# Two-layer decoder trunk on one core: scale row applied in the normalization, evictions rounded straight from the bank, loop-end products by column halves

## What is computed

```python
mod = silu(c) @ ada_w[i] + ada_b[i]
sh_a, sc_a, g_a, sh_f, sc_f, g_f = split(mod, 6)
h = rmsnorm(x, norm_mix[i]) * (1.0 + sc_a) + sh_a
x = x + g_a * mixer(h)
h = rmsnorm(x, norm_ffn[i]) * (1.0 + sc_f) + sh_f
x = x + g_f * moe(h)
```

## Time and profile before

| | |
|---|---|
| median of 3 runs | 1396.59 us (1392.68 to 1397.88) |
| profiled execution | 1399.82 us |
| its span | 1398.1 us |
| PE busy | 1323.5 us, 95% |
| DVE busy | 548.5 us, 39% |
| ACT busy | 454.5 us, 33% |
| POOL busy | 226.3 us, 16% |
| HBM read | 514.11 MB, 369 GB/s over the span |
| granted PE clock, mean | 0.983 |

### The profile page before, as it was taken

How to read it: one execution, slowest core, us unless ns; L and a number is a source line. 1 busy time by engine, 2 the same in 40 slices (tenths; PEclk the granted TensorE clock), 3 DMA queues, 4 the chain that set the end, 5 groups by cost and what they waited for, 6 DMA issues and landing times.

```text
span 1398.1 us, 33554 instructions
## 1 busy us (share of the span) xinstructions
PE 1323.5 (95%) x12029; PEld 877.8 (63%) x12030; DVE 548.5 (39%) x1263; ACT 454.5 (33%) x926; POOL 226.3 (16%) x684
## 2 busy tenths in 40 slices
PE   5899989999999999899899999999999999999986
PEld 2788675556565555445699898765555565555653
DVE  1665684323332322222644365753323233233324
ACT  3444552222222222112544554622222222222222
POOL 8200102111111211111200000021111111112110
PEclk9899999999999999999999999999999999999998
DMA  9998989999999999999996344599999999999994
GB/s 352 338 338 319 404 358 400 420 421 422 422 422 422 422 422 422 422 422 422 376 351 216 126 151 151 203 402 383 422 423 421 422 422 422 422 422 421 422 421 199
DMA packets 113979, 516.09 MB, mean 369 GB/s; under 512 B 10280, under 2 KB 47264, under 8 KB 64000
## 3 DMA queue, kind: packets, MB, share of 16 engines
q1 hardware_dynamic: 109920, 509.64, 91.0%
q0 software_dynamic: 3296, 3.50, 0.9%
q10 hardware_dynamic: 704, 2.10, 0.4%
HBM read 514.11 MB, written 1.09 MB: 369 GB/s over the span
## 4 chain that ended last, share of the span: by engine, by line
PE 65%; SPq 17%; DMA 9%; DVE 4%; ACT 2%; issue 2%; ACTq 0%; DVEq 0%
PE bank L980 17%; PE bank L1169 13%; SPq L352 8%; PE bank L1136 7%; PE bank L1095 6%; PE bank L1172 6%; PE bank L1197 6%; DMA ring<-in_exp_w_dram 6%; SPq L355 4%; PE bank L1203 3%; SPq L346 3%; DMA mods<-in_exp_w_dram 2%; PE bank L954 2%; DMA ring<-in_da_w_in_dram 2%; DVE ring_r L1472 1%
## 5 line engine op out<-in xcount | busy, mean ns | idle before, releaser
L1169 PE MATMUL bank<-ring,arena 128*64 128x512 f32 x768 | 183.9, 614 | 13.1 <-DMA ring<-in_exp_w_dram 13.1
L1136 PEld LDWEIGHTS bank<-arena 128*128 128x128 bf16 x3264 | 142.1, 98 | 55.5 <-issue 55.5
L1095 PE MATMUL bank<-arena_r 128*128 128x512 f32 x560 | 159.9, 422 | 3.0 <-DVE arena_r L1648 3.0
L1641 DVE SCALAR_TENSOR_TENSOR arena<-bank,arena 128x128 f32<-128x128 f32 x103 | 32.9, 348 | 327.5 <-ACT arena L749 327.5
L1648 DVE TENSOR_TENSOR arena_r<-bank,arena_r 128x512 fp32r<-128x512 f32 x136 | 94.1, 692 | 154.1 <-ACT arena_r L756 154.1
L1136 PE MATMUL bank<-arena 128*128 128x64 bf16 (+1 forms) x3264 | 151.8, 207 | 0.0
L749 ACT ACTIVATE arena<-bank 128x256 f32<-128x256 f32 (+1 forms) x68 | 22.6, 332 | 387.8 <-PE bank L1169 280.2
L566 POOL TENSOR_TENSOR arena<-arena,pass_base 128x2 f32 x136 | 26.2, 216 | 736.9 <-PE bank L1144 569.8
L756 ACT CAST arena_r<-bank 128x512 fp32r<-128x512 f32 x136 | 79.6, 586 | 175.3 <-PE bank L1197 112.4
L1169 PEld LDWEIGHTS bank<-ring,arena 128*64 128x64 f32 x768 | 69.0, 141 | 107.5 <-issue 101.6
L980 PE MATMUL bank<-HH_r,ring_r 128*128 128x256 f32 x448 | 127.2, 284 | 0.0
(11 more groups left out here) (277 smaller groups left out, 2168.6 us busy)
## 6 DMA issues: line engine op xcount, KB each, us to landing
ring<-in_exp_w_dram SPq DMA_DIRECT2D x264, 1024.0 KB, 24.6
ring<-in_ada_w_dram SPq DMA_DIRECT2D x48, 1024.0 KB, 12.3
mods<-in_exp_w_dram SPq DMA_DIRECT2D x40, 1024.0 KB, 25.6
HH<-in_exp_w_dram SPq DMA_DIRECT2D x40, 1024.0 KB, 21.7
arena<-in_exp_w_dram SPq DMA_DIRECT2D x40, 1024.0 KB, 26.0
ring<-in_ret_w_in_dram SPq DMA_DIRECT2D x24, 1024.0 KB, 12.0
ring<-in_da_w_in_dram SPq DMA_DIRECT2D x12, 1024.0 KB, 14.6
ring<-in_ret_w_out_dram SPq DMA_DIRECT2D x8, 1024.0 KB, 4.9
```

The costliest lines, as they stand in the source:

```text
L1095: ins = nc.tensor.matmul(banks[4 + NH * tc + hf][:, :], S[:, P * tc:P * tc + P], y[:, r, 512 * hf:512 * hf + 512], start=False, stop=(last ...
L1136: ins = nc.tensor.matmul(banks[2 - 2 * half][:, P * kk:P * kk + 2 * W], parts[:, tc, r, P * (4 * half + kk):P * (4 * half + kk + 1)], Pg[: ...
L1169: ins = nc.tensor.matmul(banks[1][W * i:W * i + W, :], xg[:, k, W * i:W * i + W], w13[j][:, k, :, :], start=(k == 0), stop=(k == KD - 1))
```

## The change

- The scale is no longer applied at the evictions of norms 1 to 3 and of the expert loop, but to `h` itself in the normalization, with a row of scales that lies on every partition (`scale_row`). The three scale rows are stored to DRAM in the order in which `h` is written, element by element (`store_scale`), and spread over the partitions (`spread_scale`). Only the shifts are loaded turned.
- At norms 1 to 3 feature block k lies in bank k mod 4. ACT rounds bank plus shift straight to `hT_hi`, DVE computes bank plus shift minus `hT_hi` straight into `hT_lo`, one block at a time. The logits go to bank 5.
- The products behind the expert loop go by column halves, and so does the update of `X` there.
- `release_ada` at norms 1 and 3 stands ahead of ACT's evictions.
- The first rounded tile of mixer 1 has another place.

```diff
@@ places of the rounded weights and of the scale rows @@
-        first_high = (mods_r[:, 3 * D:5 * D], HH_r[:, 0:2 * D], arena_r[:, 10240:12288])
+        high_before_norm = arena_r[:, 10240:12288]
+        scale_row = {1: arena[:, 5120:5120 + D], 2: gains[:, 4, :], 3: decay[:, :, :].rearrange("p h t -> p (h t)")}
...
-            return first_high[i] if (kind, l) == ("mix_in", 1) and i < 3 else high[kind, l][i % 2]
+            return high_before_norm if key == ("mix_in", 1, 0) else high[kind, l][i % 2]
...
+        def hT_count(n, k):
+            return k // 2 + 1 if n == 0 else 4 + KD * (n - 1) + k + 1
+
+        def in_bank(n, k):
+            m, half = (k // 2, k % 2) if n == 0 else (k % 4, k // 4)
+            return m, slice(T * half, T * half + T)
@@ POOL @@
+            def store_scale(n):
+                l, s = n // 2, 3 * (n % 2) + 1
+                row = browA[:, s - 2, :] if l == 0 else browB[:, s, :]
+                for q in range(4):
+                    pool.dma_start(mod_dram[l, s].rearrange("(k q p) -> q p k", q=4, k=KD)[q:q + 1],
+                                   row[32 * q:32 * q + 1, :].rearrange("a (p k) -> a p k", k=KD),
+                                   allow_slow_non_contiguous=True).then_inc(scales_stored, 16)
...
-            def turn_mods(l, first):
-                pool.dma_start(mod_T[:, l, first:first + 2, :],
-                               mod_dram[l, first:first + 2].rearrange("s (p k) -> p s k", k=KD)
-                               ).then_inc(mod_T_in[2 * l + first // 3], 16)
+            def spread_scale(n):
+                l, s = n // 2, 3 * (n % 2) + 1
+                pool.dma_start(scale_row[n], mod_dram[l, s:s + 1, :].broadcast_to([P, D])).then_inc(scale_in[n], 16)
+
+            def turn_shift(n):
+                l, s = n // 2, 3 * (n % 2)
+                pool.dma_start(mod_T[:, l, s, :], mod_dram[l, s].rearrange("(p k) -> p k", k=KD)).then_inc(mod_T_in[n], 16)
...
-            store_rows(0, 2, 3, 3)
-            store_rows(1, 0, 2, 5)
-            store_rows(1, 3, 2, 7)
+            store_rows(0, 2, 2, 3)
+            store_scale(1)
+            store_rows(1, 0, 1, 5)
+            store_scale(2)
+            store_rows(1, 3, 1, 7)
+            store_scale(3)
             pool.wait_ge(rows_stored, 192)
-            turn_mods(0, 3)
             spread(0, 2, gates_in)
-            turn_mods(1, 0)
-            turn_mods(1, 3)
+            pool.wait_ge(pv_done, DA_ITEMS)
+            pool.wait_ge(scales_stored, 16 * 4 * 3)
+            spread_scale(1)
+            for n in range(1, 4):
+                turn_shift(n)
             store_rows(0, 5, 1, 8)
             pool.wait_ge(rows_stored, 256)
             spread(0, 5, gates_in)
+            pool.wait_ge(x_new, 2)
+            spread_scale(2)
...
                     spread(1, 2, gate1_in)
+                    pool.wait_ge(s_ready, DA_ITEMS + RET_HEADS)
+                    spread_scale(3)
@@ ACT @@
             def evict_hT():
                 n = norms[0] - 1
+                if n > 0:
+                    act.wait_ge(mod_T_in[n], 16)
+                    for k in range(KD):
+                        m, at = in_bank(n, k)
+                        act.wait_ge(h_turned, 4 * n + m + 1)
+                        if k >= 4:
+                            act.wait_ge(hT_split, hT_count(n, k - 4))
+                        nc.scalar.activation(hT_hi[:, k, :], banks[m][:, at], ACT.Identity,
+                                             bias=mod_T[:, n // 2, 3 * (n % 2), k:k + 1]).then_inc(hT_rounded, 1)
+                    return
...
             def round_rw(l):
                 act.wait_ge(late_consts_in, 16 * 5)
                 act.wait_ge(rows_stored, 192)
+                act.wait_ge(scales_stored, 16 * 4 * 3)
...
             def moe(l):
                 norm_stats()
                 round_w("shared", l, 1)
+                release_ada(7 if l == 0 else 9)
                 evict_hT()
-                release_ada(7 if l == 0 else 9)
...
-                nc.scalar.activation(scoreT, banks[0][:, 0:T], ACT.Sigmoid).then_inc(scoresT_ready, 1)
+                nc.scalar.activation(scoreT, banks[5][:, 0:T], ACT.Sigmoid).then_inc(scoresT_ready, 1)
...
-                                ins = nc.scalar.activation(to, got, ACT.Identity,
-                                                           scale=mod_T[:, l, 4, k:k + 1], bias=mod_T[:, l, 3, k:k + 1])
+                                ins = nc.scalar.activation(to, got, ACT.Identity, bias=mod_T[:, l, 3, k:k + 1])
@@ PE @@
+                            k = 2 * m + kk if norms[0] == 0 else m + 4 * kk
                             ins = nc.tensor.transpose(
                                 banks[m][:, T * kk + P * tc:T * kk + P * tc + P],
-                                h[:, tc, P * (2 * m + kk):P * (2 * m + kk + 1)], ident[:, :])
+                                h[:, tc, P * k:P * (k + 1)], ident[:, :])
...
-                pe.wait_ge(u["bank0_read"], total + 1)
-                pe.wait_ge(u["bank1_read"], total + 1)
-                for tc in range(TC):
-                    for hf in range(NH):
+                for hf in range(NH):
+                    pe.wait_ge(u[f"bank{hf}_read"], total + 1)
+                    for tc in range(TC):
                         combine(tc, hf, last=True).then_inc(routed_done, 1)
@@ DVE @@
+                    else:
+                        dve.wait_ge(scale_in[n], 16)
+                        nc.vector.scalar_tensor_tensor(out=h[:, tc, :].rearrange("t (k p) -> t k p", k=KD),
+                                                       in0=X[:, tc, :].rearrange("t (p k) -> t k p", k=KD), scalar=rs[:, tc:tc + 1],
+                                                       in1=scale_row[n].rearrange("t (k p) -> t k p", k=KD),
+                                                       op0=ALU.mult, op1=ALU.mult).then_inc(h_ready, 1)
...
             def evict_hT():
                 n = norms[0] - 1
+                if n > 0:
+                    dve.wait_ge(mod_T_in[n], 16)
+                    for k in range(KD):
+                        m, at = in_bank(n, k)
+                        dve.wait_ge(hT_rounded, hT_count(n, k))
+                        nc.vector.scalar_tensor_tensor(out=hT_lo[:, k, :], in0=banks[m][:, at], scalar=mod_T[:, n // 2, 3 * (n % 2), k:k + 1],
+                                                       in1=hT_hi[:, k, :], op0=ALU.add, op1=ALU.subtract).then_inc(hT_split, 1)
+                    return
...
-                                ins = nc.vector.tensor_scalar(to, got, mod_T[:, l, 4, k:k + 1], mod_T[:, l, 3, k:k + 1],
-                                                              ALU.mult, ALU.add)
+                                ins = nc.vector.tensor_scalar(to, got, mod_T[:, l, 3, k:k + 1], None, ALU.add)
...
-                update_x(5, [(routed_done, TC * NH * l + n + 1) for n in range(TC * NH)])
+                update_x(5, [(n % TC, n // TC, routed_done, TC * NH * l + n + 1) for n in range(TC * NH)])
```

More of the change, by code:

```diff
@@ L1043, in moe @@
                     hT_there(k)
-                    ins = product(banks[0][:, 0:T], (rw_hi[:, k, :], rw_lo[:, k, :]), [x[:, k, :] for x in hTs],
+                    ins = product(banks[5][:, 0:T], (rw_hi[:, k, :], rw_lo[:, k, :]), [x[:, k, :] for x in hTs],
                                   k == 0, k == KD - 1)
@@ L1485, in evict @@
+                def evict(m):
+                    dve.wait_ge(h_turned, m + 1)
+                    for k in (2 * m, 2 * m + 1):
+                        ins = nc.vector.tensor_scalar(hT_full[:, k, :], banks[m][:, in_bank(0, k)[1]],
+                                                      mod_T[:, 0, 1, k:k + 1], mod_T[:, 0, 0, k:k + 1], ALU.mult, ALU.add)
                     ins.then_inc(hT_dve, 1)
                 def low(m):
-                    dve.wait_ge(hT_rounded, 4 * n + m + 1)
+                    dve.wait_ge(hT_rounded, m + 1)
@@ new lines, in evict_hT, with update_x @@
+                for m in range(4):
+                    low(m)
+            def update_x(gate, parts_done):
+                for n, (tc, hf, done, count) in enumerate(parts_done):
+                    dve.wait_ge(done, count)
+                    ins = nc.vector.tensor_tensor(h[:, tc, 512 * hf:512 * hf + 512], banks[4 + NH * tc + hf][:, :],
+                                                  gains[:, gate, 512 * hf:512 * hf + 512], ALU.mult)
+                    if hf == NH - 1:
+                        step(ins)
+                        nc.vector.tensor_tensor(X[:, tc, :], X[:, tc, :], h[:, tc, :], ALU.add).then_inc(x_new, 1)
@@ L1803, in _ @@
             dve.wait_ge(gates_in, 16)
-            update_x(2, [(first_rows_out, n + 1) for n in range(TC * NH - 1)] + [(out_done, 4)])
+            update_x(2, [(n // NH, n % NH, first_rows_out, n + 1) for n in range(TC * NH - 1)] + [(TC - 1, NH - 1, out_done, 4)])
             moe(0)
@@ L1871, in _ @@
             dve.wait_ge(gate1_in, 16)
```

(2 more changed lines are left out.)

53 lines of the change are left out of this document (16 added, 37 removed).

## The result

The changed kernel took 1422.78 us (median of 4 runs), the kernel before 1395.63 us (4 runs). The ratio is 1.019 (95% interval 1.017 to 1.021), so the change costs about 27 us (24 to 29 us) where I had forecast a gain of 2.6 us, and the time lies 22 us above the range. The profiled run took 1421.17 us (span 1419.3).

The account below looks back on a forecast made before the run. The prediction took full DMA to bound the expert loops, so only shorter paths through the norms count. Terms 2.3 - 1.6 - 1.4 - 0.7 - 0.9 - 0.3 + 0 gave -2.6 us, 1394.0 us, range 1389.5 to 1400.5.

Parts of the forecast that it names:

- Part 5: Scale row's stores and spreads ahead of the first shared weight tile: start of norm 1 later by 2.3 us.
- the second rival: Stores cost 3.9 us a scale, the first shared tile comes 12.6 us late: +7 us, 1403.6 us; chance 0.08.
- The scale row in the normalization: Normalization of norms 1 to 3: 1186 ns instruction becomes 1284 ns, one of two on the path, +0.1 us.
- Part 1: Evictions of h straight from the bank: -1.6 us at norm 1, -1.4 us at norm 3, nothing at norm 2.
- Part 2: End products by column halves, last addition 0.85 us sooner: -0.7 us at norm 2, -0.9 us at the kernel's end.
- Part 4: Ring release ahead of the evictions: DMA hole at 192 to 198 us fills, another opens before `sh_up`; 0 us.
- The third rival: Early ring release is a real gain: first stream ends 4.8 us sooner, 1389.2 us; chance 0.08.
- Part 3: Expert loops: ACT's evictions lose an operand, DVE's a second operation; -0.3 us, the rest beside the full DMA.

Follow-up runs that it names:

- a_plain: The changed kernel with each scale stored in the order it lies, four contiguous 1 KB stores, and the row read strided; 1397.53 us, ratio 0.9997.
- e_runs: The changed kernel with VectorE permuting the scale row in SBUF first and POOL storing 128 B runs, 96 pieces instead of 3072; 1398.03 us, ratio 0.9998.
- j_sp_stores: The kernel before plus twelve stores of 256 single elements, issued by SyncE from the loads' own queue into an unread DRAM tensor; 1429.62 us, ratio 1.0236.
- b_halves: The kernel before with only the end products of both expert loops by column halves and the update in that order; 1394.59 us, ratio 0.9981.
- g_contig_all: f_contig2 carried to all three norms, bf16 parts kept in that order, so gathering products read weights at a 16 B stride; 1411.06 us, ratio 1.0104.
- e_release_late: a_plain with the ring released behind the evictions again; 1398.16 us, ratio 1.0005.
- f_contig2: a_plain with X, scale row and h walked contiguously in the second norm alone, h turned with weights at a 32 B stride; 1393.32 us, ratio 0.9969.
- f_again: f_contig2 run once more, the same kernel, against the kernel before; 1395.03 us, ratio 0.9978.

## Why the prediction was wrong

**Part 5, the term that failed: mis-sized, and its upper bound too.** I had 0.78 us a scale, with bounds 0 and 3.9; it is 8.2 us. The mechanism, its place and the tile were right, and the second rival told it (a late shared tile, all norms' gain eaten), with a chance of 0.08 and a price under half of the true one. Two steps led there:
- The nearest row was gn, single elements that are read, and I took its price for stores. 2048 elements read cost 1.6 us by my estimate from the dip around their landing, 0.8 ns apiece, with other small loads beside them; 3072 stored cost 24.7 us, 8 ns apiece. Reads were not tried alone, but their row was no guide to the store.
- The upper bound, 61 ns a piece on one of 16 engines, came from the packets of POOL's queue, as if a packet were a piece. It is not: the page counts 4112 packets in that queue for the changed kernel, for a_plain and for e_runs alike, though they differ by 3072 single elements (the queue's row is the same in all three but for its share, 1.2 or 1.3%).
The rule of the Trainium skill that I weighed (DMA: Bandwidth & Descriptors, Rules for kernel authors) is one descriptor per element. The loads' own queue agrees: the page of the profile of j_sp_stores counts 3096 more packets under 512 B than the kernel before, for 3072 elements. For POOL's queue no row shows it. The prediction said by that rule that the sum turns, and then gave the case 0.08. Where a rule speaks against a part and no row shows the operation, the bound should have stayed open.

**The scale row in the normalization, a term that I had at 0.1 us.** I took the two-source row at 1284 ns, which is that of the last norm, where everything is contiguous, for an instruction that walks X at a stride. It takes 2.1 us. The view by line and shape does not show strides; the code does. At norms 1 and 3 both instructions lie on the path, not one of two: from the last addition of X to ACT's first eviction are 4.73 us before, 6.32 us after, and 4.90 us in g_contig_all, where everything is contiguous. So the +0.1 would have been right for the contiguous form (4.90 - 4.73), and the strided one costs 1.6. At norm 2 it is a part of the difference between -0.7 and what came, beside PE's clock (0.51 during the transposes): last addition to first product 8.64 us before, 703.36 to 712.71, 9.35 us, after.

**Part 1, the evictions: -1.6 and -1.4 forecast, about -1.1 each found, and that lost to the normalization.** ACT and DVE do their part as costed (eight of ACT's evictions in 3.03 us, 0.37 each; DVE's in 3.23 us). But the pace of 0.213 us a product, which carried the term, was that of one execution. There the granted clock over the stretch was 0.83, a mix of the two levels; in b_halves, with the same norm code, it was 1.00. The row for 192 to 202 us of the kernel before, then of b_halves:

```profile
192.00:202.00 10.00, 6.74 (x39) 5.98 (x39) 7.53 (x12) 8.43 (x14) 1.03 (x3) 0.83 0.55 199
```

```profile
192.00:202.00 10.00, 6.65 (x54) 5.44 (x47) 8.40 (x13) 9.70 (x16) 0.00 (x0) 1.00 0.53 197
```

From the last addition of X to the sigmoid the old form takes 12.6 us in the first execution and 11.25 us in the second (189.60 to 200.85). At the same full clock the change and a_plain take 11.7 us (norm 1 of the one, norm 3 of the other) and g_contig_all, with the new evictions and a contiguous normalization, 10.3 us. So at full clock the evictions are worth some 1.0 us a norm and not 1.6, the 2.1 us normalization costs 1.4 us, and the new form is 0.45 us slower than the old. ACT's list is what binds there, in the old form and in the new, and not PE's products (timeline of ACT, b_halves, then the changed kernel):

```profile
194.34 1.02 ACT L646 ACTIVATE mods<-bank,mod_T 128x256 f32<-128x256 f32 x2 [0.21 <-PE bank L967]
...
199.44 1.28 ACT L715 ACT_TABLE_LOAD   x1
200.74 0.20 ACT L715 ACTIVATE lexp<-ident 128x1 f32<-128x1 f32 x1
200.85 0.37 ACT L717 ACTIVATE arena<-bank 128x256 f32<-128x256 f32 x1
```

```profile
219.71 3.03 ACT L677 ACTIVATE HH_r<-bank,mod_T 128x256 fp32r<-128x256 f32 x8 [1.78 <-PE bank L1006]
...
223.69 1.28 ACT L754 ACT_TABLE_LOAD   x1
...
225.10 0.37 ACT L756 ACTIVATE arena<-bank 128x256 f32<-128x256 f32 x1
```

The sigmoid follows ACT's own work without a wait. In the change PE's last logit product ends at 224.19, 0.9 us earlier. From ACT's first eviction to the sigmoid are 6.51 us in the old form and 5.39 in the new, 1.1 us less. The step that failed is the one where I took 18 products at 0.213 us from a single execution as the pace of the stage. The prediction also said that evictions gain nothing at norm 2, from a row at the low level; in b_halves, at the high one, the mixer's first product waits 0.84 us for DVE's old eviction.

**Part 2 right.** 0.85 us at each loop end, as forecast, and b_halves measures 0.9981, 2.7 us less with an interval of 0.6 to 4.8, which holds the forecast 1.7.

**Part 4 right.** The hole at 192 to 198 fills (126 to 416 GB/s), another opens ahead of `sh_up`, and the time is the same (1.0005 against 0.9997). The third rival falls. (In the changed kernel itself the dips have put this stage elsewhere; the reading is from a_plain and e_release_late.)

**Part 3** (-0.3 us) was not tried alone. The groups became shorter (ACT 456 to 369 ns, DVE 405 to 344 ns at 128x128) where a loop of full DMA hides them.

**The sum without the stores** was -4.9 us, or -4.0 us with the 0.9 us of spread and turned loads that Part 5 also held; a_plain, which is that sum, gives 0.9997, -0.4 us with an interval of -2.4 to +1.5. The difference fits the two points above, Part 1 and the 2.1 us instruction. f_contig2 is at -4.3 us and f_again at -3.1, near the forecast, but that is no confirmation of it: norms 1 and 3 are there as in a_plain, and norm 2 is 2.0 us shorter in the trace, so more was gained than these parts explain. Where the rest comes from stays open.

## What to carry to other kernels

Count the pieces of a DMA, not its bytes: 12 KB in 3072 pieces cost as much of a full load stream as 10 MB of weights, and a small permutation on an engine ahead of each store (`e_runs`) makes the cost too small to measure. When an operand is folded into an existing instruction, look at how the other operands are walked, and take the price from a row with the same strides, since the view by shape does not show them. And read a pace only together with the granted clock of its stretch: a term that rests on the slow level of one execution may not exist in the next.

## What the runs showed that I had not expected

- Single-element stores to DRAM from POOL's queue: 8 ns apiece over all 16 engines together (24.7 us for 3072), where I had estimated 0.8 ns for single-element reads; the DMA share reads 1.0 over each whole dip, so it is the GB/s column that shows them.
- The packet counts of POOL's software queue do not show pieces: 4112 with and without the 3072. In the loads' own hardware queue they do: the page of j_sp_stores has 13376 packets under 512 B where the kernel before has 10280, 3096 more.
- SyncE is held 3.2 us by the issue of one store of 256 single elements (38.41 us for twelve); POOL's timeline has 0.59 us for one of its own (2.34 us for four).
- A stride of 32 B costs ScalarE's cast a factor of two (2146 against 1058 ns), VectorE's two-source forms 0.7 to 0.9 us at 128x1024, VectorE's one-source form some 0.4 us by an estimate, and TensorE's fp32 weights little (eight transposes in 1.17 us, where the contiguous ones of norm 1 took 1.09); bf16 weights at 16 B go from 98 to 160 ns.
